# The order of three partial products inside a unit of weights, and where the unit waits for its low half

## The reference

```python
def first_block(...):            # once
    h = rms_norm(x, mix_norm_g);  proj = h @ w_in        # 1024 -> 7184
    ... mLSTM, neighbourhood attention, cross attention to mem ...
    merged = g_ml * (y_ml @ w_br_ml) + g_na * (y_na @ w_br_na) + g_xa * (y_xa @ w_br_xa)
    x = x + merged @ w_out
    x = x + conv_glu_ffn(rms_norm(x, ffn_norm_g), ...)   # 1024 -> 2 * 2816 -> 1024
def second_block(...):
    x = x + short_conv_mixer(rmsnorm(x, ..), a_w_in, a_conv, a_w_out)
    x = x + conv_ffn(rmsnorm(x, ..), ...)                # 1024 -> 2 * 2816 -> 1024
    ... forgetting attention over 8 pairs of heads; kv and qg from x ...
    x = x + o @ b_w_out
    x = x + conv_ffn(rmsnorm(x, ..), ...)
```

## Time and profile before

| | |
|---|---|
| median of 2 runs | 2243.19 us (2242.39 to 2244.0) |
| profiled execution, its own time | 2244.19 us |
| span of the core in it | 2242.4 us |
| mean granted clock of TensorE | 0.988 |
| TensorE busy | 2172.6 us, 97% of the span |
| GpSimd, VectorE, ScalarE busy | 1180.1, 1021.8, 867.6 us |

### The profile page before, as it was taken

One profiled execution on the slowest core, in us unless ns is written; L12 is line 12 of the kernel. 1 busy time (PEld: TensorE's weight loads), 2 busy tenths in 40 slices (PEclk: granted clock), 3 DMA queues, 4 the chain that ended last, 5 costly groups with the idle time before them and its releaser, 6 DMA issues.

```text
span 2242.4 us, 30457 instructions
## 1 busy us (share of the span) xinstructions
PE 2172.6 (97%) x9968; PEld 1747.3 (78%) x9968; DVE 1021.8 (46%) x1710; ACT 867.6 (39%) x1270; POOL 1180.1 (53%) x1572
## 2 busy tenths in 40 slices
PE   6989999799999999999999999999999999999999
PEld 5867666588888888888878888886777768888887
DVE  5466587633344554124445555214555554555400
ACT  6334323443344343331234434324444454443421
POOL 7433322676755655655556565655333325555653
PEclk9989999899999999999999999999999999999999
DMA  6213311133323233323232333331322212333332
GB/s 217 88 48 108 113 53 33 52 98 101 110 90 101 95 94 96 104 82 113 85 104 85 103 94 92 102 96 57 123 76 76 76 43 89 99 98 98 94 103 71
DMA packets 61479, 205.06 MB, mean 91 GB/s; under 512 B 6848, under 2 KB 6976, under 8 KB 61392
## 3 DMA queue, kind: packets, MB, share of 16 engines
q1 hardware_dynamic: 61200, 203.65, 29.4%
q10 hardware_dynamic: 192, 0.30, 0.1%
HBM read 201.52 MB, written 2.39 MB: 91 GB/s over the span
## 4 chain that ended last, share of the span: by engine, by line
PE 87%; DVE 6%; ACT 2%; DVEq 2%; issue 1%; POOL 1%; DMA 1%; ACTq 0%; SPq 0%
PE bank L1309 27%; PE bank L1311 27%; PE bank L1310 27%; PE bank L1517 1%; PE bank L1581 1%; PE bank L1557 1%; PE bank L1350 1%; PE bank L1532 1%; POOL YL L461 0%; DMA RAW<-in_w_att 0%; PE bank L1446 0%; ACT WH L493 0%; DVEq L814 0%; DVE SS L791 0%; PE bank L1388 0%
## 5 line engine op out<-in xcount | busy, mean ns | idle before, releaser
L405 POOL TENSOR_TENSOR WL<-RAW,WH 128x256 fp32r<-128x256 f32 x1496 | 1151.3, 803 | 1030.2 <-ACT WH L493 1029.2
L1309 PE MATMUL bank<-XH,WH 128*128 128x512 f32 x1840 | 729.1, 396 | 2.9 <-DVE XQ L830 2.0
L1311 PE MATMUL bank<-XH,WL 128*128 128x512 f32 x1840 | 717.6, 390 | 0.0
L1310 PE MATMUL bank<-XL,WH 128*128 128x512 f32 x1840 | 717.5, 390 | 0.0
L493 ACT ACTIVATE WH<-RAW 128x1024 fp32r<-128x1024 f32 x374 | 392.2, 1052 | 233.7 <-PE bank L1311 209.5
L1309 PEld LDWEIGHTS bank<-XH,WH 128*128 128x128 f32 x1840 | 346.5, 188 | 81.7 <-issue 5.5
L1310 PEld LDWEIGHTS bank<-XL,WH 128*128 128x128 f32 x1840 | 346.3, 188 | 74.0 <-issue 3.1
L1311 PEld LDWEIGHTS bank<-XH,WL 128*128 128x128 f32 x1840 | 346.2, 188 | 72.8
L1309 PE MATMUL bank<-FH,WH 128*128 128x512 f32 x528 | 205.4, 389 | 0.0
L1310 PE MATMUL bank<-FL,WH 128*128 128x512 f32 x528 | 205.4, 389 | 0.0
L1311 PE MATMUL bank<-FH,WL 128*128 128x512 f32 x528 | 205.4, 389 | 0.0
(11 more groups left out here) (274 smaller groups left out, 2295.1 us busy)
## 6 DMA issues: line engine op xcount, KB each, us to landing
RAW<-in_w_up SPq DMA_DIRECT2D x132, 512.0 KB, 3.5
RAW<-in_w_att SPq DMA_DIRECT2D x47, 512.0 KB, 3.5
RAW<-in_w_down SPq DMA_DIRECT2D x48, 448.0 KB, 3.3
RAW<-in_w_fa SPq DMA_DIRECT2D x32, 512.0 KB, 3.5
RAW<-in_w_down SPq DMA_DIRECT2D x24, 512.0 KB, 3.5
RAW<-in_w_ain SPq DMA_DIRECT2D x24, 512.0 KB, 3.5
RAW<-in_w_mrg SPq DMA_DIRECT2D x18, 512.0 KB, 3.6
RAW<-in_w_mrg SPq DMA_DIRECT2D x22, 256.0 KB, 2.7
```

The lines of the kernel that those rows point to most:

```text
L405: last = nc.gpsimd.tensor_tensor(WL[:, s, w], RAW[:, s, w], WH[:, s, w].bitcast(F32), ALU.subtract)
L1309: mm(dst[:, 0:width], WH[:, s, w], a, start=start and k == 0, stop=False)
L1310: mm(dst[:, 0:width], WH[:, s, w], b, start=False, stop=False)
L1311: last = mm(dst[:, 0:width], WL[:, s, w], a, start=False, stop=stop and k == kc - 1)
```

## The change

The loop over blocks and the three matmuls inside change places. A unit now runs all blocks with high x high, then all with weights high x activations low, then all with weights low x activations high. It starts after `hi_ready` instead of `lo_ready`, and waits for `lo_ready` ahead of the third pass. The waits for the activations' blocks and the call of `halfway` stand in the first pass alone.

```diff
             s = (u0 + j) % NSLOT
-            pe.wait_ge(lo_ready, i * per + (u0 + j + 1))
-            for k in range(kc):
-                if halfway and k == kc // 2:
-                    halfway()
-                if ready:
-                    pe.wait_ge(ready[0], ready[1] + k + 1)
-                w = slice(k * P, (k + 1) * P)
-                a, b = xh[:, k0 + k, 0:width], xl[:, k0 + k, 0:width]
-                mm(dst[:, 0:width], WH[:, s, w], a, start=start and k == 0, stop=False)
-                mm(dst[:, 0:width], WH[:, s, w], b, start=False, stop=False)
-                last = mm(dst[:, 0:width], WL[:, s, w], a, start=False, stop=stop and k == kc - 1)
+            pe.wait_ge(hi_ready, i * per + (u0 + j + 1))
+            for n, (w_, x_) in enumerate(((WH, xh), (WH, xl), (WL, xh))):
+                if n == 2:
+                    pe.wait_ge(lo_ready, i * per + (u0 + j + 1))
+                for k in range(kc):
+                    if halfway and n == 0 and k == kc // 2:
+                        halfway()
+                    if ready and n == 0:
+                        pe.wait_ge(ready[0], ready[1] + k + 1)
+                    last = mm(dst[:, 0:width], w_[:, s, k * P:(k + 1) * P], x_[:, k0 + k, 0:width],
+                              start=start and n == 0 and k == 0, stop=stop and n == 2 and k == kc - 1)
             last.then_inc(unit_done, 1)
```

## The result

| | before | after |
|---|---|---|
| median of 2 runs | 2243.19 us (2242.39 to 2244.0) | 2277.95 us (2277.72 to 2278.19) |
| profiled execution, its own time | 2244.19 us | 2278.19 us |
| span | 2242.4 us | 2276.4 us |
| mean granted clock | 0.988 | 0.984 |

The ratio is 1.0154, with a 95% interval of 1.0138 to 1.0171: clearly slower, by less than 2%.

What follows compares the result with a forecast made beforehand. TensorE, busy 97% of the span, was taken to bound the kernel. Waiting +23.7, clock +10.5, branch units -0.5 and +0 made +33.7 on 2244.19, or 2277.9; the median 1.0 lower, called 2277 us, range 2258 to 2290.

Steps and rivals of the forecast that it cites:

- Part 1: Nine borders where the last activation split is needed last: 17 matmuls behind it instead of 3, 23.7 us lost.
- the formula T + 4.03: End of a border's unit after the change, T being the end of VectorE's last split: 0.05 + 0.80 + 14 x 0.227.
- Part 2: TensorE's clock falls to half behind new holes at the nine borders, 1.5 us per fall: 10.5 us lost.
- The bound of 13.5 for nine falls: Upper bound of the clock's cost if it falls at all nine borders; 17 if the two longest cost double.
- Part 3: Removed waits for GpSimd's low halves: 0 in the memory's units, bounds -2.5 and +2.5; -0.5 us at the branch units.
- 1.9 gained and 2.2 lost: Memory's units: a unit ends 1.9 us earlier after its low half, but the run of low halves comes 2.2 later.
- One of the listed signs: In the profile after, TensorE's waits for WL, GpSimd's low half, were to move to the third pass.
- Part 4: Every unit: the wait in mid-unit and the new order of weights cost 0, bounds +-1 ns a matmul, +-8.5 us.
- The rival of a clock that holds: At the borders the clock holds through short holes, so only the 23.7 us remains: 2266 us, chance 0.20.
- The one in which all nine fall: The clock falls at all nine borders, twice over at the long ones: 2286 us, chance 0.12.
- The gain from the waits removed: Start and branches: the 25.9 us waited for low halves comes back; 2252 with falls, 2242 without, chance 0.05.
- the change of pace: Every matmul runs at another pace through weight loads or evener reading, 8.5 us per ns on 8544 matmuls; chance 0.05.

Runs made afterwards that it cites:

- the first six experiments: Six variants of the unit's order, its low-half wait or its holes; medians 2244.15, 2280.6, 2242.74, 2280.38, 2255.64 and 2269.54 us.
- the first: Changed kernel, but units that wait for activations block by block keep the old order and old wait: 2244.15 us, ratio 1.0004 to the kernel before.
- third: Kernel before, old block order in every unit, but the low half is awaited ahead of its first low matmul: 2242.74 us, ratio 0.9995.
- eighth: Kernel before with the late low-half wait and, at aout, the second unit's first three blocks ahead of the first unit's last: 2242.27 us, ratio 0.999.
- ninth: As the eighth, but each of the two aout units awaits its bank and low half only at its own first block: 2241.72 us, ratio 0.9991.
- the fourth experiment: Changed kernel, new order in every unit, but the low half awaited at the unit's start as before: 2280.38 us, ratio 1.016.

## Why the prediction was right

The forecast was 2277, the median 2277.95, and the theory's expected time held in each of the first six experiments, but for the 1 to 2 us that the first was to gain at the start. By the prediction's own steps:

- **Part 1, 23.7 us of waiting.** The filled holes measure six of its terms without the clock: 3.2, 2.6, 3.2, 3.2, 2.55, 2.6 against 3.1, 2.53, 3.18, 3.17, 2.53, 2.53. f, where the changed kernel kept its clock, cost 2.55. Right to 0.1 us each. Two terms were added up wrongly and cancel: by the formula T + 4.03, out comes to 599.95 against the next unit's old start at 596.77, a loss of 3.2 and not 3.1; and at bout 1836.74 + 2.13 is 1838.87 and not 1838.97, a loss of 1.95 and not 2.05. bout and fa can't be parted from their falls. bout's chain ran as worked out: its last split ended 5.4 us behind the unit's start, where the corrected sum gives 5.47.
- **Part 2, 10.5 us for the clock.** Too small: the clock fell at eight of the nine borders, not at seven, the longest hole and fa cost more than one share (2.1 at aout; 2.7 at fa, its later units included), and the usual price was 1.6 us, not 1.5. Taking Part 1 from the account by place leaves 14.2 us. At fa the kernel before had falls as well, at 1552.3 and 1566.0, which its own times hold already; the changed kernel has one stretch of half clock more there. The bound of 13.5 for nine falls was passed, that of 17 was not.
- **Part 3, nothing at the start.** The memory's part ended 0.2 us from where it did. The first unit ended at 19.1 us, ahead of the forecast 19.8. The chain at the start is as it was drawn: the longer first unit held back the scale, and ScalarE's high half behind the scale held back GpSimd. ScalarE's and GpSimd's rows after, beside the earlier trace rows:

```profile
19.76 0.47 ACT L511 ACTIVATE TE<-bank,EPSC 128x256 f32<-128x256 f32 x1 [1.90 <-PE bank L1321]
```

```profile
24.26 30.90 POOL L405 TENSOR_TENSOR WL<-RAW,WH 128x256 fp32r<-128x256 f32 x36 [3.00 <-ACT WH L493]
```

  Both are 1.4 us later, where 2.2 was worked out. But the 0 came out for another reason than the one given, 1.9 gained and 2.2 lost. One of the listed signs failed: the waits for WL were to move to the third pass, and there are none. What sets the end of the memory's part, in both kernels, is VectorE, which from some 22 us on goes almost without a break through the splits of x and, in between, the reads of their banks. One such read and the last split of x, before:

```profile
27.05 0.42 DVE L828 TENSOR_TENSOR MK<-bank,RM 128x256 f32<-128x256 f32 x1
...
40.65 1.22 DVE L792 SCALAR_TENSOR_TENSOR XL<-X,PAR,XH 128x512 fp32r<-128x512 f32 x1
```

  and after, with the unit that waited for this bank:

```profile
27.31 0.42 DVE L828 TENSOR_TENSOR MK<-bank,RM 128x256 f32<-128x256 f32 x1
...
40.91 1.23 DVE L792 SCALAR_TENSOR_TENSOR XL<-X,PAR,XH 128x512 fp32r<-128x512 f32 x1
...
27.80 1.22 PE L1310 MATMUL bank<-MH,WH 128*128 128x256 f32 x8 [2.32 <-DVE MK L828]
```

  VectorE's row moved by 0.3 us only. Before, the same unit started at 27.69, put down to GpSimd, though its bank had come free only at 27.47: the two conditions were due at nearly the same time, and taking the one away uncovered the other. The next wait, for TC at 39.81 after, ends on VectorE's row too. The branch units gave 0.7 us against 0.5.
- **Part 4, no cost in the row.** Experiments 1 and 3, and the 0.227 us of the rows above.
- **What wasn't in the sum: -3.2 us ahead of the branch units.** Unit for unit the difference arises at falls. The stretch 57.30 to 60.60, at half clock in the earlier trace rows, is at full clock after:

```profile
57.30:60.60 3.30, 3.30 (x16) 2.73 (x15) 0.00 (x0) 0.00 (x0) 3.30 (x7) 1.00 0.24 96
28.90:32.30 3.40, 3.40 (x18) 3.40 (x18) 3.17 (x5) 2.66 (x4) 3.40 (x4) 0.50 0.52 157
```

  and 28.90 to 32.30 has a fall instead. Up to the branch units the kernel before spends 23.9 us at half clock and the one after 17.1; half of the difference is 3.4. The change need not have caused this. The third, eighth and ninth experiments run the same instructions up to aout, and their profiled executions spend 23.9, 13.6 and 13.7 us at half clock ahead of the branch units and start out 0.2, 4.0 and 5.5 us earlier than the kernel before. So executions of one and the same code differ by 5 us in this part. The kernel before alone ran from 2238.5 to 2249.6 us over all its executions. Two terms of the sum were thus off by 3.7 and 3.2 us and cancelled. That the total came within 1 us of the forecast is luck; what its parts earned is an error of 3 to 4 us, well inside the range.
- **Small slips that change nothing.** The spread of 2268 to 2286 is 2 us wider at each end than its two terms give (three falls, 4.5, and 2.5 of part 3). At -9 ns a matmul the time would be 2200, not quite 2% faster. And GpSimd's low halves are done up to 23 us ahead of their units in fa and up to 40 at bout, not 11 at most.

The rival of a clock that holds was wrong: behind eight of nine holes it fell. The one in which all nine fall was nearer to the clock's true term than the forecast was. The gain from the waits removed was refuted by the fourth experiment, the change of pace by the first.

## What to carry to other kernels

Where a consumer takes its inputs block by block as they are finished, count the work that stands behind the last input, not only ahead of it: reordering a loop from block-major to pass-major moves (passes - 1) x (blocks - 1) instructions from the cover to the tail, here 14 matmuls or 3.2 us at each border. A wait that ends last is worth removing only if the next condition behind it (here the bank that VectorE reads) isn't due at the same time. And a hole in TensorE's row cost more than its length here: beside 2.5 to 3.2 us of waiting came mostly 1.6 of half clock, which matmuls for nothing in the hole took back.

## What the hardware showed that wasn't expected

- Filling a hole with useless matmuls at six places made the changed kernel 8.4 us faster. The granted clock then stayed at 1.00 at all six. The Trainium skill, TensorE: Matmul & The Clock Gate, HAM oscillation, tells of a kernel in which every group of matmuls starts cold, at the lower clock, behind a wait for data of some 3 to 5 us. The trace agrees at the three borders with holes that long or nearly (2.96, 3.46 and 4.83 us), and goes further than the page: it shows a fall behind holes of 2.25 us at three borders of four.
- A hole of the same length (2.25 us, waiting for XL) was followed by a fall at up0, up1 and up2 and not at f in the changed kernel, and with the same order and the others filled it fell at f. So the length of a hole by itself doesn't settle it, and one execution can't tell what the clock costs to better than a fall or two.
- After the longest hole (4.83 us at aout) the stretch from 1141.7 to 1148.4 shows 0.50 throughout; part of it lies in the hole itself, so it cost 2.1 us and not twice 1.6.
